# Expert FFN in seven steps of 512 hidden columns instead of four of 896, in a two-block float32 kernel

## The reference, cut to what matters

```python
def swiglu(t, w_gate, w_up, w_down):
    return (silu(t @ w_gate) * (t @ w_up)) @ w_down      # 1024 -> 3584 -> 1024

def moe_swiglu(h, router_w, w_gate, w_up, w_down):
    logits = t @ router_w
    top_v, top_i = top_k(logits, 2)                      # 2 of 8 experts a token
    gates = one_hot(top_i, 8) weighted by softmax(top_v)
    for e in range(8):
        out = out + gates[:, e] * swiglu(t, w_gate[e], w_up[e], w_down[e])
```

## Time and profile before

| | |
|---|---|
| median of three runs | 2924.63 us (2921.05 to 2924.83) |
| span of the profiled execution, first to last instruction | 2916.6 us, 8.0 us under the median |
| expert stage (first expert matmul at 1874.70 us) | about 1000 us of it |
| PE busy | 2840.0 us, 97% |
| DVE, ACT, POOL busy | 1941.0, 1623.0, 462.5 us |
| DMA | 679.12 MB, mean 233 GB/s |

### The profile page before, as it was taken

One profiled execution on the slowest core, in us unless ns is written; L12 is line 12 of the kernel. 1 busy time (PEld: TensorE's weight loads), 2 busy tenths in 40 slices (PEclk: granted clock), 3 DMA queues, 4 the chain that ended last, 5 costly groups with the idle time before them and its releaser, 6 DMA issues.

```text
span 2916.6 us, 42979 instructions
## 1 busy us (share of the span) xinstructions
PE 2840.0 (97%) x18565; PEld 2640.4 (91%) x18578; DVE 1941.0 (67%) x1967; ACT 1623.0 (56%) x1787; POOL 462.5 (16%) x215
## 2 busy tenths in 40 slices
PE   8999999999999999999999999999999999999997
PEld 7999999999999999989899988899898989889886
DVE  5677647766676567735467624487877878777774
ACT  4555446554555465522477512476767667677763
POOL 1000000001000000000000000133333333333332
PEclk9999999999999999989999989899999999999998
DMA  7645456726445477551688731399999999999993
GB/s 231 172 145 174 145 194 235 265 81 180 152 136 181 136 260 246 166 156 59 204 293 293 233 106 53 130 371 337 369 335 350 351 351 358 336 368 333 349 356 126
DMA packets 355543, 679.12 MB, mean 233 GB/s; under 512 B 17265, under 2 KB 237713, under 8 KB 355217
## 3 DMA queue, kind: packets, MB, share of 16 engines
q1 hardware_dynamic: 339712, 616.49, 60.7%
q0 software_dynamic: 15632, 59.80, 6.4%
HBM read 675.19 MB, written 4.69 MB: 233 GB/s over the span
## 4 chain that ended last, share of the span: by engine, by line
PE 82%; DVE 9%; ACT 6%; issue 2%; DMA 1%; POOL 0%; SPq 0%; DVEq 0%; ACTq 0%
PE bank L568 79%; DVE w_lo L1364 4%; ACT w_hi L1953 3%; DVE ring_tail L1323 1%; PE bank L1189 1%; ACT ring_tail L2005 1%; PE bank L664 1%; PE bank L689 1%; DVE ring_tail L1325 1%; DVE gates L1377 1%; DMA ring_head<-in_w_in 0%; DVE ring_low L1293 0%; PE bank L715 0%; PE bank L640 0%; DMA ring_head<-in_w_mix_out 0%
## 5 line engine op out<-in xcount | busy, mean ns | idle before, releaser
L1859 DVE TENSOR_TENSOR ew_lo<-ring_head,ew_hi 128x1792 fp32r<-128x1792 f32 (+1 forms) x288 | 680.5, 2395 | 199.6 <-ACT ew_hi L2271 199.6
L2271 ACT CAST ew_hi<-ring_head 128x1792 fp32r<-128x1792 f32 (+2 forms) x384 | 647.1, 1694 | 274.7 <-PE bank L568 274.7
L549 POOL TENSOR_TENSOR ew_lo<-ring_head,ew_hi 128x1792 fp32r<-128x1792 f32 (+1 forms) x96 | 388.7, 4049 | 859.3 <-ACT ew_hi L2271 859.3
L568 PE MATMUL bank<-xs_hi,ring_low 128*128 128x256 f32 x1984 | 388.9, 282 | 0.0
L568 PE MATMUL bank<-x_hi,w_hi 128*128 128x256 f32 x1152 | 323.4, 287 | 15.3 <-DVE w_lo L1364 14.9
L1364 DVE TENSOR_TENSOR w_lo<-ring_head,w_hi 128x2048 fp32r<-128x2048 f32 x108 | 247.5, 2292 | 126.2 <-ACT w_hi L1953 126.2
L568 PE MATMUL bank<-x_hi,w_lo 128*128 128x256 f32 x1152 | 318.4, 283 | 0.0
L568 PE MATMUL bank<-x_lo,w_hi 128*128 128x256 f32 x1152 | 318.4, 283 | 0.0
L568 PEld LDWEIGHTS bank<-xs_hi,ring_low 128*128 128x128 f32 x1984 | 313.3, 188 | 0.7
L568 PE MATMUL bank<-ew_hi,xe_hi 128*128 128x448 f32 x1024 | 295.1, 370 | 4.4 <-DVE ew_lo L1859 4.4
L568 PE MATMUL bank<-ew_lo,xe_hi 128*128 128x448 f32 x1024 | 291.6, 366 | 0.0
(11 more groups left out here) (391 smaller groups left out, 5799.4 us busy)
## 6 DMA issues: line engine op xcount, KB each, us to landing
ring_head<-in_moe_w_gate SPq DMA_DIRECT2D x128, 896.0 KB, 6.6
ring_head<-in_moe_w_up SPq DMA_DIRECT2D x128, 896.0 KB, 6.8
ring_head<-in_moe_w_down SPq DMA_DIRECT2D x96, 1024.0 KB, 7.0
ring_head<-in_w_in SPq DMA_DIRECT2D x76, 1024.0 KB, 5.6
ring_tail<-in_ada_w POOLq DMA_DIRECT2D x48, 1024.0 KB, 7.3
ring_head<-in_ffn_w_in SPq DMA_DIRECT2D x44, 1024.0 KB, 6.6
ring_head<-in_ffn_w_out SPq DMA_DIRECT2D x22, 1024.0 KB, 8.3
ring_head<-in_xa_kv SPq DMA_DIRECT2D x16, 1024.0 KB, 5.4
```

Of the source, the lines that this page charges most:

```text
L549: pool.tensor_tensor(ew_lo[:, h, 0:n], ring(c % 6)[:, 0:n], ew_hi[:, h, 0:n].bitcast(F32), ALU.subtract).then_inc(w_used[c % 6], 1)
L568: ins = nc.tensor.matmul(out, lhsT, rhs, start=start, stop=stop, **kw)
L1859: v.tensor_tensor(ew_lo[:, h, 0:n], ring(c % 6)[:, 0:n], ew_hi[:, h, 0:n].bitcast(F32), ALU.subtract).then_inc(w_used[c % 6], 1)
L2271: a.copy(ew_hi[:, c % DEPTH_HI, 0:n], ring(c % 6)[:, 0:n]).then_inc(f.count(part_hi), 1)
```

## The change

`EC` becomes 512: seven steps of 512 hidden columns, one bank for gate and one for up, 4 transposes a turn. A gate or up matrix of a step comes in two parts of four k-tiles x 512 columns (rows of 2048 bytes), a down matrix in two parts of two k-tiles; every part is 128 x 2048, 1 MB, and an expert has 42. Which of the four `ew` buffers a part uses, and whether POOL splits it, now goes by `(e * 42 + c) % 4`, so it shifts by two from expert to expert. The places of `form`, `finish` and `results` in the lists move to match.

```diff
-EC = 896
+EC = 512
 ETILES = EC // P
-EHALF = EC // 2
+WK = CH // EC
...
-PARTS = [(kind, s, i) for kind, s in EXPERT_PARTS for i in range(4)]
-FIRST = {(kind, s): 4 * n for n, (kind, s) in enumerate(EXPERT_PARTS)}
+PARTS = [(kind, s, i) for kind, s in EXPERT_PARTS for i in range(2)]
+FIRST = {(kind, s): 2 * n for n, (kind, s) in enumerate(EXPERT_PARTS)}
...
-        both = tiles(banks[:, 6:8, :].rearrange("p b c -> p (b c)")[:, 0:EC], ETILES)
+        both = tiles(bank[6], ETILES)
...
-                                    part = kpn(wd[0, e, step * EC:(step + 1) * EC, :])[:, 2 * i:min(2 * i + 2, ETILES), :]
+                                    part = kpn(wd[0, e, step * EC:(step + 1) * EC, :])[:, 2 * i:2 * i + 2, :]
...
-                                    part = kpn((wg if kind == "gate" else wu)[0, e])[:, 2 * i:2 * i + 2, step * EC:(step + 1) * EC]
+                                    part = kpn((wg if kind == "gate" else wu)[0, e])[:, WK * i:WK * i + WK, step * EC:(step + 1) * EC]
...
-                        h = c % DEPTH_HI
+                        h = (e * len(PARTS) + c) % DEPTH_HI
                         f.bump(part_hi)
-                        if c % 4 == 3:
+                        if h == 3:
                             pool.wait_ge(part_hi, f.now(part_hi))
-                            pool.tensor_tensor(ew_lo[:, h, 0:n], ring(c % 6)[:, 0:n], ew_hi[:, h, 0:n].bitcast(F32),
+                            pool.tensor_tensor(ew_lo[:, h, :], ring(c % 6), ew_hi[:, h, :].bitcast(F32),
                                                ALU.subtract).then_inc(w_used[c % 6], 1)
...
+                    def widen(e, kind, step, b):
+
+                        for i in range(2):
+                            hi, lo = part(e, FIRST[kind, step] + i, WK)
+                            for k in range(WK):
+                                t = WK * i + k
                                 for x, w, last in ((xe_hi, hi, False), (xe_hi, lo, False), (xe_lo, hi, True)):
-                                    for n in range(2):
-                                        mm(bank[b + n][:, 0:EHALF], x[:, t, :], w[:, k, n * EHALF:(n + 1) * EHALF],
-                                           t == 0 and w is hi and x is xe_hi, t == KD - 1 and last,
-                                           part_done if last and (k, n) == (1, 1) else None)
+                                    mm(bank[b][:, :], x[:, t, :], w[:, k, :], t == 0 and w is hi and x is xe_hi, t == KD - 1 and last,
+                                       part_done if last and k == WK - 1 else None)
...
-                        v.tensor_tensor(tiles(eact, 2), tiles(esilu, 2), banks[:, 2:4, 0:EHALF], ALU.mult).then_inc(f.count(turn_ready), 1)
+                        v.tensor_tensor(eact, esilu, bank[2], ALU.mult).then_inc(f.count(turn_ready), 1)
...
-                                    if c == FIRST["up", s] + 7:
-                                        form(base + FIRST["up", s] + 4)
-                                low(c)
-                                if (kind, i) == ("up", 3) and step:
+                                    if c == FIRST["up", s] + 5:
+                                        form(base + FIRST["up", s] + 2)
+                                low(e, c)
+                                if (kind, i) == ("down", 0) and step < STEPS - 1:
                                     finish()
-                                if e and c == FIRST["up", 0] + 7:
+                                if e and c == FIRST["up", 0] + 5:
                                     results((2, 3))
-                                if e and c == FIRST["up", 0] + 8:
+                                if e and c == FIRST["up", 0] + 6:
                                     results((0, 1))
...
-                                    if c == FIRST["gate", s] + 7:
+                                    if c == FIRST["gate", s] + 5:
                                         if s:
                                             finish()
                                         form()
```

More of the change, by code:

```diff
@@ L542, in experts @@
                 for e in range(EXPERTS):
[L543 to L545 removed]
+                    for c in range(len(PARTS)):
+                        h = (e * len(PARTS) + c) % DEPTH_HI
                         f.bump(part_hi)
[L547 removed]
+                        if h == 3:
                             pool.wait_ge(part_hi, f.now(part_hi))
[L549 removed]
+                            pool.tensor_tensor(ew_lo[:, h, :], ring(c % 6), ew_hi[:, h, :].bitcast(F32),
                                                ALU.subtract).then_inc(w_used[c % 6], 1)
@@ L1166, in gather, with part @@
                                        t == 0, t == 1, gather_full if (i, t) == (3, 1) else None)
-                    def part(c, k, n):
+                    def part(e, c, k):
                         pe.wait_ge(w_used[c % 6], f.next(w_used[c % 6]))
[L1171 to L1178, removed]
+                        return [tiles(t[:, (e * len(PARTS) + c) % DEPTH_HI, :], k) for t in (ew_hi, ew_lo)]
+                    def widen(e, kind, step, b):
[3 more added lines that the diff above has]
+                                t = WK * i + k
                                 for x, w, last in ((xe_hi, hi, False), (xe_hi, lo, False), (xe_lo, hi, True)):
-                                    for n in range(2):
-                                        mm(bank[b + n][:, 0:EHALF], x[:, t, :], w[:, k, n * EHALF:(n + 1) * EHALF],
-                                           t == 0 and w is hi and x is xe_hi, t == KD - 1 and last,
-                                           part_done if last and (k, n) == (1, 1) else None)
+                                    mm(bank[b][:, :], x[:, t, :], w[:, k, :], t == 0 and w is hi and x is xe_hi, t == KD - 1 and last,
+                                       part_done if last and k == WK - 1 else None)
                     def turn():
@@ L1190, in turn, with down @@
                         ins.then_inc(f.count(turned), 1)
-                    def down(step):
+                    def down(e, step):
                         pe.wait_ge(eact_ready, f.next(eact_ready))
-                        for i in range(4):
-                            tops = range(2 * i, min(2 * i + 2, ETILES))
-                            hi, lo = part(FIRST["down", step] + i, len(tops), D)
+                        for i in range(2):
+                            tops = range(2 * i, 2 * i + 2)
+                            hi, lo = part(e, FIRST["down", step] + i, 2)
                             for t in tops:
@@ L1236, in experts @@
                                 pe.wait_ge(gate_silu, f.next(gate_silu))
-                                widen("gate", step, 0)
+                                widen(e, "gate", step, 0)
                                 if e and step == 1:
@@ L1244, in experts @@
                                     f.bump(result_free, 4)
-                                down(step - 1)
+                                down(e, step - 1)
                             pe.wait_ge(gate_silu, f.next(gate_silu))
@@ L1848, in _, with low @@
                     v.tensor_scalar(crowded[:, :], crowd[:, 0:1], float(P), None, ALU.is_gt).then_inc(f.count(crowd_ready), 1)
[L1850 to L1855, removed]
+                    def low(e, c):
+                        h = (e * len(PARTS) + c) % DEPTH_HI
+                        if h == 3:
                             f.bump(part_hi)
@@ L1858, in low @@
                         dve.wait_ge(part_hi, f.next(part_hi))
-                        v.tensor_tensor(ew_lo[:, h, 0:n], ring(c % 6)[:, 0:n], ew_hi[:, h, 0:n].bitcast(F32),
+                        v.tensor_tensor(ew_lo[:, h, :], ring(c % 6), ew_hi[:, h, :].bitcast(F32),
                                         ALU.subtract).then_inc(w_used[c % 6], 1)
@@ L2262, in _, with high @@
                         take(4 + q, htok[:, q // 2, 512 * (q % 2):512 * (q % 2) + 512], bank[4 + q][:, :])
-                    def high(c, done):
-                        kind, step, i = PARTS[c]
-                        n = 2 * EC if kind != "down" else D * (min(2 * i + 2, ETILES) - 2 * i)
+                    def high(e, c, done):
                         if done > 0:
@@ L2270, in high @@
                         eng.wait_ge(ffn_loaded[c % 6], f.next(ffn_loaded[c % 6], 16))
-                        a.copy(ew_hi[:, c % DEPTH_HI, 0:n], ring(c % 6)[:, 0:n]).then_inc(f.count(part_hi), 1)
+                        a.copy(ew_hi[:, (e * len(PARTS) + c) % DEPTH_HI, :], ring(c % 6)).then_inc(f.count(part_hi), 1)
                     def form():
-                        a.activation(tiles(esilu, 2), banks[:, 0:2, 0:EHALF], ACT.Silu).then_inc(f.count(gate_silu), 1)
+                        a.activation(esilu, bank[0], ACT.Silu).then_inc(f.count(gate_silu), 1)
                     def finish():
```

10 lines of the change are left out of this document (5 added, 5 removed).

## The result

The changed kernel is slower by 0.4%: 2928.91 us (median of 20 runs) against 2917.39 us for the kernel before (20 runs on the same chips), ratio 1.0041 [1.0033, 1.005], some 12 us. One of the 20 runs of the kernel before took 4652.7 us, and the ratio leaves it out. The forecast of 2922.5 stood on a median of three runs of the kernel before that was itself high. Over more runs the kernel before has 2917.39 us, and the profiled execution of the changed kernel took 2935.61 us for a span of 2933.8. So 1.8 us lie around a span, not 8.0, and with them the profiled execution of before took about 2918.4 us.

What follows compares the result with a forecast made beforehand. PE was taken to set the pace, with DMA close behind. Terms of -13.0, +1.2, +8.8, +1.5, +0.5 and -1.1 sum to -2.1 us, giving 2922.5 us; the 8-in-10 range is 2910 to 2944.

Steps and rivals of the forecast that it cites:

- Splits, steady state: Mid-expert: cast plus POOL split take 6.8 us of 8.16, DVE at worst 6.4, so the moves cost nothing.
- the line through both gives 4.7 us for 2048: POOL's split time for 2048 elements, extrapolated from 4.38 us for 1792 and 3.40 for 1024.
- matmuls and turns: Gate and up in fewer, wider matmuls: -13.0 us for eight experts; transposes in 7 groups instead of 4: +1.2 us.
- rival 4: Gate and up: matmuls in a row into one bank are slower, from 233 ns the gain is gone, 2935 us; 5%.
- the boundary: Between experts PE stands 0.4 us for part 0, 1.5 more for POOL's part 1 at four boundaries: +8.8 us.
- Rival 1: Between experts the stall is covered, leaving only the -12 us gain, 2912 us; 20%.
- DMA: Weight loads in 2 KB rows run at a lower rate, 352 GB/s, about matching PE's pace: +1.5 us.
- rival 2: Expert's second half: DMA becomes the bound, 2936 us at 95 ns a 2 KB packet, about 2950 at 97; 25%.
- the ring stands full: At a boundary part 6 is issued only at +10 us, so 3 us or so of each expert are lost to DMA.
- the clock: Last expert: PE's wait shortens by some 1 us, -1.1; should the clock stay at 2.4 GHz, 2.8 us more saved.
- rival 3: Between experts the clock falls after PE's waits, +11 us, 2934 us; 12%.
- The 8.0 us around it: Time outside the profiled span, implied by a median of 2924.63 us, added to the span of 2914.5 us.

Runs made afterwards that it cites:

- e7: The changed kernel with each POOL split issued as two instructions of 1024 columns; 2982.36 us, ratio 1.0219 to the kernel before.
- e8: The changed kernel with DVE's split replaced by the landed part times 1.0, one input instead of two (product loses its meaning); one run, 2904.44 us.
- e6: The kernel before (896 columns a step) with all 48 splits of an expert on DVE; 2926.3 us, ratio 1.0029.
- e5: The changed kernel with all splits on DVE and the next expert's first two casts and splits put ahead of the boundary work; 2899.99 us, ratio 0.9935.
- e2: The changed kernel with gate and up parts read as 256 rows of 4096 bytes, so other weights reach the products; 2930.24 us, ratio 1.0041.
- e1: The changed kernel with all 42 splits of an expert on DVE, none on POOL; 2908.14 us, ratio 0.9967 to the kernel before.

## Why the prediction was right or wrong

**Wrong: "Splits, steady state ... These moves cost nothing".** This term was 0 and measured +19.1 us, some 18 of them POOL's. Its step that failed is "the line through both gives 4.7 us for 2048", used as the time of every split. The two means, 4.38 us for 1792 and 3.40 for 1024 elements, each held waiting for DVE: by itself a split of 1024 takes 2.38 us (e7) and one of 2048 takes 4.62 (e8). 4.7 us was thus right for POOL alone, by luck (the line takes 1.27 ns an element from the means, and the two own durations give 2.19), and wrong for POOL beside DVE, where it is 5.99 us at the mean. The forecast took the exclusion in one direction only, as DVE waiting for POOL, and gave DVE 4.3 us for it, which takes up to 6.01. The other direction has the smaller slack: 1.9 for the cast, 4.5, up to 2.0 of a running DVE split and 0.2 make 8.6 us where PE leaves 8.16. The forecast named the consequence ("what POOL is late is what PE stands") without a price for it.

The Trainium skill (SBUF — State Buffer, Who interferes with whom) has a rule for it: a DVE instruction with two SBUF inputs contends with a GpSimd instruction that reads SBUF, and whoever issues first has the shared port pair for its whole instruction. The traces agree in both directions: POOL 6.55 us behind a running DVE split and 4.50 without its rest, DVE mostly 4.9 to 6.0 us behind POOL against 2.28. The three cases in which a queued DVE split passes a POOL split that began before it (at 2175.50, DVE's at 2175.95) don't fit the rule as it is put there. The same section counts a `tensor_scalar` in a two-port mode among those that contend, which fits the up to 3.93 us in e8.

**Why now and not before.** The two splits meet in both kernels: 83 of 84 POOL splits start during a DVE one now, and 95 of 96 did before. Here is one of those of the kernel before, with its cast and the DVE splits at its start:

```profile
2062.56 1.70 ACT L2271 CAST ew_hi<-ring_head 128x1792 fp32r<-128x1792 f32 x1 [0.74 <-PE bank L568]
...
2060.96 3.95 DVE L1859 TENSOR_TENSOR ew_lo<-ring_head,ew_hi 128x1792 fp32r<-128x1792 f32 x2
...
2064.34 4.52 POOL L549 TENSOR_TENSOR ew_lo<-ring_head,ew_hi 128x1792 fp32r<-128x1792 f32 x1 [5.18 <-ACT ew_hi L2271]
```

DVE has 2060.96 + 3.95 - 2064.34 = 0.57 us to go, POOL takes 3.95 us more than that, and from the start of the cast it is 6.30 us. For the 64 splits of 1792 elements this is 6.09 us at the median and 6.77 at most, and three parts of 12 matmuls give 36 x 0.2027 = 7.30 us: enough. Now it is 7.94 us at the median and over 8.16 in 36 of 84, of which not each keeps PE waiting. POOL's own time has grown by 0.5 us, the cast by 0.2, and what is left of the DVE split from 0.39 to 1.45 us at the median, while the slack has grown by 0.86. Before, PE was full, and POOL's help was worth 9 us (e6).

**Right: matmuls and turns.** -11.8 predicted, -12.2 measured (e5). The spacing of 512 columns in one bank is 227.1 ns; rival 4 is out.

**Right: the boundary.** PE's part 0 came 0.36 us late, from the starts 2135.13 and 2135.95 less two intervals (0.4 predicted), and part 1 of odd experts 2012.11 - 2010.33 - 0.227 = 1.55 us (1.5 predicted). Rival 1 is out. There POOL begins 0.45 us before DVE's split ends (2007.16 against 2007.61) and takes 4.89 us, which is why 4.7 us served well. Part 3 of the even experts, which stands behind the boundary too, the forecast didn't price; it is among the +19.1.

**Wrong but small: DMA.** +1.5 us predicted, 0 measured, at a DMA share of 0.95 where 0.97 or more was foretold. The packet of 2048 bytes took 91.7 ns at the mean against 93 estimated, below the 94 at which rival 2 began; e2 shows that even that time doesn't matter, and e5 runs at 354 GB/s over the whole stretch. That "the ring stands full" at a boundary costs nothing that PE sees.

**Right: the clock.** It stays at 1.00 from 1900 to 2850 us, rival 3 is out. At the last step PE stands 1.18 us instead of 2.98, and the 12 pairs behind it start 5.12 us / 11 = 0.465 us apart, nearly the full pace of 0.453: the 2.8 us that the forecast gave in case the clock stays were saved, and the wait is 1.8 us shorter, not 1.1. Another 2 us the first expert saves in e1, where the forecast had lost 0.5. Cast and split are longer by 0.5 us as foretold (PE waits 4.89 us for them against 4.41), but the gather takes 5.18 us instead of 6.69, and the matmuls behind it come to their full pace some 1 us sooner. Why the pace differs there, no run here shows.

**Wrong: the base.** "The 8.0 us around it" are 1.8 us. On that base the forecast's own sum means 2916.3 us against 2918.4, while the change gave +12. That 2922.5 came near 2928.91 is luck: a base 6 us too high and ends that saved 6 us more than forecast stood against a term 19 us too low.

Two small sums in the rivals are off, and nothing hangs on them: 42 x 2.72 + 3 is 117.2 and not 117.6, and 129.5 us is 3.2 more than 126.29 and not 3.5.

## What to carry to other kernels

When an engine's duration is taken from means beside another engine, first split them: look at single instructions, and at what the neighbour was doing at their start. For two engines that exclude each other, the slack of each must hold its own work plus the rest of the other's, in both directions. Here they met at nearly every split before and after the change; what the change took away was the room for it. Here a helper engine that took a quarter of the splits cost 21 us (e1 against the changed kernel) although both engines were free part of the time, and the gain of the wider matmuls appeared in part when it was taken out (e1, 0.9967) and in full when the next expert's first casts were moved ahead as well (e5, 0.9935).

## What the runs showed of the hardware that was not expected

- POOL's and DVE's fp32 splits run one after the other as whole instructions. Each takes its own 4.5 or 2.28 us plus what is left of the other's, and in 3 of 84 cases a second, queued DVE split also goes ahead of the waiting POOL one. DVE's product from PSUM (0.67 us at 2201.44, in the middle of POOL's split) is not held.
- With POOL's instruction cut in halves the kernel was 2.2% slower than the kernel before and 1.8% slower than the changed one (e7): DVE goes in between, and a pair lasts up to 9.20 us instead of 4.76.
- More splits on DVE made DVE less busy: 776.55 us of 900 without POOL (e1) against 797.50 with it, since a held instruction counts as busy.
- A stand of PE of 1.18 us or 1.39 us, and in e7 of 2.53 and 2.58 us, was followed by matmuls at nearly full pace; after 2.98 us, 3.51 us (e7) and 4.12 us (e6) they were at about half.
